# First norm and first dense products in halves of features, squares summed on VectorE and GpSimd, weight splits behind reciprocals: a four-layer diffusion block on one Trainium2 core

## What is computed

```python
def rms_norm(x, gain):
    y = x32 * lax.rsqrt(jnp.mean(x32 * x32, axis=-1, keepdims=True) + EPS)
def modulate_norm(x, gain, shift, scale):
    return rms_norm(x, gain) * (1 + scale) + shift
for i in range(DEPTH):
    mx = jnp.split((silu_c @ ada_w[i] + ada_b[i])[:, None, :], 6, axis=-1)
    hx = modulate_norm(xs, norm_mix[i], mx[0], mx[1])
    ... token mixer: dense products, head norms or convolution, dense product ...
    xs = xs + mx[2] * yx
    hx = modulate_norm(xs, norm_ffn[i], mx[3], mx[4])
    xs = xs + mx[5] * conv_ffn(hx, ffn_w_up[i], ffn_w_dw[i], ffn_b_dw[i], ffn_w_down[i])
```

## Time and profile before

| | |
|---|---|
| median of three runs | 2537.51 us |
| the profiled execution | 2537.72 us |
| its span | 2535.9 us |
| instructions | 35941 |
| TensorE (PE) busy | 2439.2 us, 96% |
| VectorE (DVE) busy | 1808.4 us, 71% |
| ScalarE (ACT) busy | 1044.8 us, 41% |
| GpSimd (POOL) busy | 671.4 us, 26% |
| read from HBM | 334.95 MB, 132 GB/s |

### The profile page before, as it was taken

The page is one execution under the profiler, slowest core; times in us unless marked ns, Lnnn a source line. Parts: engine busy times, 40 slices in busy tenths (PEclk is TensorE's granted clock), DMA queues, the critical chain, the costliest instruction groups (busy, mean ns, idle before and its releaser), DMA issues. The chain is left out here.

```text
span 2535.9 us, 35941 instructions
## 1 busy us (share of the span) xinstructions
PE 2439.2 (96%) x12542; PEld 1994.7 (79%) x12542; DVE 1808.4 (71%) x2642; ACT 1044.8 (41%) x1641; POOL 671.4 (26%) x458
## 2 busy tenths in 40 slices
PE   6998899999999999999999998989999999998999
PEld 4774488888888856788888887868888888767999
DVE  4876559888974344427888768987988876855774
ACT  3335634443232223314444327863544323345443
POOL 5213233332300020032333324854333224101000
PEclk8998999999999999999999999999999999999999
DMA  7542025545633311233555542203455545312555
GB/s 269 180 159 74 1 91 167 174 167 193 220 106 100 101 65 50 83 99 133 174 171 168 179 145 75 67 24 118 169 171 174 185 163 132 109 50 67 184 183 181
DMA packets 94888, 337.46 MB, mean 133 GB/s; under 512 B 11840, under 2 KB 13632, under 8 KB 94656
## 3 DMA queue, kind: packets, MB, share of 16 engines
q1 hardware_dynamic: 67136, 240.38, 28.1%
q10 hardware_dynamic: 24768, 86.74, 10.3%
q0 software_dynamic: 2880, 8.92, 1.7%
HBM read 334.95 MB, written 1.05 MB: 132 GB/s over the span
## 5 line engine op out<-in xcount | busy, mean ns | idle before, releaser
L647 PE MATMUL bank<-Hhi,Whi 128*128 128x512 f32 (+1 forms) x2440 | 873.0, 358 | 29.4 <-DVE Hlo L1535 13.5
L648 PE MATMUL bank<-Hlo,Whi 128*128 128x512 f32 (+1 forms) x2440 | 859.7, 352 | 0.0
L649 PE MATMUL bank<-Hhi,Wlo 128*128 128x512 f32 (+1 forms) x2440 | 859.7, 352 | 0.0
L1448 DVE TENSOR_TENSOR Wlo<-raw,Whi 128x1024 fp32r<-128x1024 f32 x424 | 633.4, 1495 | 253.8 <-ACT Whi L1098 245.0
L1098 ACT ACTIVATE Whi<-raw 128x1024 fp32r<-128x1024 f32 x424 | 448.2, 1059 | 769.6 <-DMA raw<-in_weights 717.6
L647 PEld LDWEIGHTS bank<-Hhi,Whi 128*128 128x128 f32 x2440 | 464.7, 190 | 104.3 <-issue 28.0
L648 PEld LDWEIGHTS bank<-Hlo,Whi 128*128 128x128 f32 x2440 | 465.2, 191 | 64.0 <-issue 3.4
L649 PEld LDWEIGHTS bank<-Hhi,Wlo 128*128 128x128 f32 x2440 | 464.8, 191 | 61.5
L527 POOL TENSOR_TENSOR cond_w<-cond_w,cond 128x1024 f32<-128x1024 f32 x107 | 259.2, 2422 | 621.5 <-DVE square L1472 514.5
L647 PE MATMUL bank<-Ghi,Whi 128*128 128x512 f32 (+1 forms) x770 | 269.1, 350 | 0.0
L649 PE MATMUL bank<-Ghi,Wlo 128*128 128x512 f32 (+1 forms) x770 | 267.1, 347 | 0.0
(11 more groups left out here) (242 smaller groups left out, 2990.7 us busy)
## 6 DMA issues: line engine op xcount, KB each, us to landing
raw<-in_weights SPq DMA_DIRECT2D x424, 512.0 KB, 3.3
cond_w<-in_ada ACTq DMA_DIRECT2D x160, 512.0 KB, 3.9
ada_raw<-in_ada SPq DMA_DIRECT2D x16, 512.0 KB, 15.3
ada_ring<-in_ada SPq DMA_DIRECT2D x16, 512.0 KB, 7.9
rel_in<-in_rpb POOLq DMA_DIRECT2D x48, 128.0 KB, 6.3
decay_t<-in_dist POOLq DMA_DIRECT2D x4, 640.0 KB, 4.2
X<-in_x ACTq DMA_DIRECT2D x1, 2048.0 KB, 10.5
out_y<-X SPq DMA_DIRECT2D x1, 1024.0 KB, 4.8
```

Of the source, the lines that this page charges most:

```text
L647: t.matmul(dst, Whi[:, st.slot, w], hi, start=start, stop=False)
L648: t.matmul(dst, Whi[:, st.slot, w], lo, start=False, stop=False)
L649: return t.matmul(dst, Wlo[:, st.slot, w], hi, start=False, stop=stop)
L1448: v.tensor_tensor(Wlo[:, st.slot, :], raw[:, st.slot, :], Whi[:, st.slot, :].bitcast(F32), ALU.subtract)\
```

## The change

Nothing is computed otherwise; order and places change.

- **Start.** SP loads slices 0 and 2, the four weight slots, then slices 1 and 3. ACT loads the table for Sqrt early and squares all eight chunks into `first_squares`; DVE adds chunks 0 to 3 and POOL 4 to 7 (before: POOL squared and added seven). `first_scale` and `first_chunks` make H for features 0 to 3 from slices 0 and 2; then slices 1 and 3 are stored, and features 4 to 7 follow. TensorE's `first_tiles` does chunks 0 to 3 of four tiles around slices 1 and 3, and chunks 4 to 7 after. Transposes of the identity (`idle_products`) stand where it waits. The banks are FIRST_BANKS, and ACT's QK loop of layer 0 is written out.
- **QK loops:** ACT's root and DVE's `normed` stand ahead of the split of the same step. In layer 0 the ring slice's rows are copied at m = 2 in the first round too.
- **Attention of layer 0:** DVE makes the two late splits one step later; ACT's stay.
- **Retention:** the split for gate tile 4 is done with head 3; TensorE's first o tile waits for each chunk of Y by itself.
- **Convolution:** `diagonals(0)` stands behind Uhi of round 0; 16 `keep_warm` products stand ahead of the last mean, 24 instead of 30 behind it.
- **Last feed-forward:** 8 idle products ahead of `norm_spread`, 10 behind.

```diff
+FIRST_SLICES = (0, 2, 1, 3)
+FIRST_BANKS = (5, 6, 6, 4)
...
-            for q in range(16):
-                sp.dma_start(ada_raw[:, q, :], ada[q, :, :]).then_inc(first_ada[q], 16)
-            for s in range(SLOTS):
-                sp.dma_start(raw[:, s, :], weights[s, :, :]).then_inc(raw_loaded[s], 16)
+            for nth, piece in enumerate(FIRST_SLICES):
+                if nth == 2:
+                    for s in range(SLOTS):
+                        sp.dma_start(raw[:, s, :], weights[s, :, :]).then_inc(raw_loaded[s], 16)
+                for q in range(4 * piece, 4 * piece + 4):
+                    sp.dma_start(ada_raw[:, q, :], ada[q, :, :]).then_inc(first_ada[q], 16)
...
+                pool.wait_ge(first_squared, c + 1)
+                if c > 5:
+                    pool.wait_ge(first_added_too, c - 5)
+                g.tensor_tensor(first_squares[:, c, :], first_squares[:, c - 1, :], first_squares[:, c, :], ALU.add)\
+                    .then_inc(first_added_too, 1)
 
             for layer, p in enumerate(layers):
...
+            def idle_products(count, b=7):
+
+                for n in range(count):
+                    t.transpose(bank[b][:, 0:P], ident[:, :], ident[:, :])
...
+            def first_slice(nth, idle=0):
+                if nth >= 2:
+                    pe.wait_ge(rows_copied, nth)
+                for k in range(C):
+                    q = 4 * FIRST_SLICES[nth] + k // 2
+                    if k % 2 == 0:
+                        idle_products(idle, 3)
+                        pe.wait_ge(first_ada[q], 16)
+                    last = ada_product(bank[FIRST_BANKS[nth]], k, ada_raw[:, q, 512 * (k % 2):512 * (k % 2) + 512])
+                last.then_inc(ada_rows_made, 1)
...
+            def first_tiles(p, steps):
+
+                pe.wait_ge(tile_free, p["mix_tile"] + 4)
+                for k in range(4):
+                    for m in range(2):
+                        first_tile(steps[m], m, (k,))
+                    if k == 1:
+                        first_slice(2)
+                ada_cols(2)
+                first_tile(steps[2], 2, range(4))
+                first_slice(3)
+                first_tile(steps[3], 3, (0, 1))
+                ada_cols(3)
+                first_tile(steps[3], 3, (2, 3))
+                for k in range(4, C):
+                    for m in range(2):
+                        first_tile(steps[m], m, (k,))
+                first_tile(steps[2], 2, range(4, C))
...
-                pe.wait_ge(tile_free, FREE0 + p["mix_tile"] + 48)
                 groups = [[(Step(p["o"] + 2 * m), 8), (Step(p["o"] + 2 * m + 1), 8)] for m in range(C)]
                 for m in range(C - 1):
-                    tile(p["mix_tile"] + 48 + m, m, groups[m], Yhi, Ylo, ALL)
+                    tile(p["mix_tile"] + 48 + m, m, groups[m], Yhi, Ylo, ALL,
+                         (tile_free, FREE0 + p["mix_tile"] + 32) if m == 0 else None)
...
                 for c in range(C):
+                    if c == C - 1:
+                        keep_warm(16)
                     mean_of(c)
...
-                keep_warm(30)
+                keep_warm(24)
...
                 if last_layer:
                     norm_sum(r, tok)
+                    idle_products(8)
                     norm_spread(r, tok)
+                    idle_products(10)
...
+                last.then_inc(cond_spread, 1)
+            first_slice(0)
+            ada_cols(0)
+            pe.wait_ge(cond_ready, 2)
+            first_slice(1, 3)
+            first_norm_sum()
+            ada_cols(1)
+            idle_products(4, 3)
             norm_spread(0, ALL)
-            ada_cols(3)
+            idle_products(8, 3)
```

On ACT and DVE:

```diff
                             act.wait_ge(weights_used, st.n + 1)
                             a.activation(na_sq[:, m % 2, tok], bank[m][:, tok], ACT.Square).then_inc(qk_squared, 1)
-                            split(st)
                             if m:
                                 root_of(m - 1, k - 1, tok)
+                            if layer or st.n:
...
                     a.preload_act_table(ACT.Sqrt)
+                    if h == 3:
+                        split(Step(p["g"] + 1))
...
-                diagonals(0)
                 for c in range(C):
...
                     a.activation(Uhi[:, k, :, CONV_PAD:CONV_PAD + CTX], U[:, k, :, CONV_PAD:CONV_PAD + CTX],
                                  ACT.Copy).then_inc(u_hi, 1)
+                    if c == 0:
+                        diagonals(0)
...
-            square_last(0, ALL)
+            a.preload_act_table(ACT.Sqrt)
             for r in range(2):
                 act.wait_ge(cond_spread, r + 1)
                 for k in range(2):
                     last = a.activation(cond[:, r, 512 * k:512 * (k + 1)], bank[2 * r + k][:, :], ACT.Copy)
                 last.then_inc(cond_ready, 1)
+            act.wait_ge(x_loaded, 16)
+            for c in range(C):
+                a.activation(first_squares[:, c, :], X[:, c, :], ACT.Square).then_inc(first_squared, 1)
+            act.sem_inc(last_squared, 2)
             root_of_norm(0, ALL)
-            for n in range(LEAD):
-                split(Step(n - LEAD))
+            split(Step(-LEAD))
+            split(Step(1 - LEAD))
+            for c in range(C):
+                for half, hs in halves(ALL):
+                    act.wait_ge(norm_scaled, 2 * c + half + 1)
+                    a.activation(Hhi[:, c, hs], ring[(2 * c + half) % 4][:, hs], ACT.Identity,
+                                 bias=mod[:, 0, c, half:half + 1]).then_inc(h_hi, 1)
+                if c < 2:
+                    split(Step(c + 2 - LEAD))
             for layer, p in enumerate(layers):
```

```diff
+            def first_store(nth):
+                dve.wait_ge(ada_rows_made, nth + 1)
+                v.tensor_copy(rows[:, :], bank[FIRST_BANKS[nth]][:, :]).then_inc(rows_copied, 1)
+                ada_store(nth, FIRST_SLICES[nth])
...
+            def first_chunks(first, end, splits):
...
+                for c in range(first, end):
+                    for half, hs in halves(ALL):
+                        n = 2 * c + half
+                        if n >= 4:
+                            dve.wait_ge(h_ready, n - 3)
+                        v.scalar_tensor_tensor(ring[n % 4][:, hs], X[:, c, hs], scale[:, 0, c, half:half + 1],
+                                               spread_bank(0, ALL)[:, hs], ALU.mult, ALU.mult).then_inc(norm_scaled, 1)
+                        if half:
+                            low(n - 1)
+                    low(2 * c + 1)
+                    if c < len(splits):
+                        split(splits[c])
...
-                            if layer == 0 and 0 < n < ADA_QK and m == 2:
+                            if layer == 0 and n < ADA_QK and m == 2:
                                 ada_rows(n)
                             if layer == 0 and n < ADA_QK and m == 3:
                                 ada_store(ADA_START + n)
                             if m:
                                 normed(m - 1, k - 1, i, tok)
+                            if layer or k:
+                                split(Step(p["mix"] + 8 * nth + m, 4, i))
...
-                    if s in LATE_SPLITS[:late]:
-                        split(Step(p["v"] + 8 - late + LATE_SPLITS.index(s)))
+                    if s - 1 in LATE_SPLITS[:late]:
+                        split(Step(p["v"] + 8 - late + LATE_SPLITS.index(s - 1)))
...
                     if h + 1 < RET_HEADS:
                         weighted_scores(h + 1)
+                    if h == 3:
+                        split(Step(p["g"] + 1))
...
-            for s in range(ADA_START):
-                dve.wait_ge(ada_rows_made, s + 1)
-                v.tensor_copy(rows[:, :], bank[5 + s % 2][:, :]).then_inc(rows_copied, 1)
-                ada_store(s)
-                if s == 2:
-                    invert_root(0, ALL)
+            for c in range(1, 4):
+                dve.wait_ge(first_squared, c + 1)
+                if c > 1:
+                    dve.wait_ge(first_added, c - 1)
+                v.tensor_tensor(first_squares[:, c, :], first_squares[:, c - 1, :], first_squares[:, c, :], ALU.add)\
+                    .then_inc(first_added, 1)
+            first_store(0)
+            first_store(1)
+            invert_root(0, ALL)
             dve.wait_ge(const_loaded, CONSTS_IN)
             v.tensor_scalar(qk_gain[:, :, 0:1], qk_gain[:, :, 0:1], NA_HD ** -0.5, None, ALU.mult)
-            for n in range(LEAD):
-                split(Step(n - LEAD))
+            first_scale(0, first_scaled)
+            split(Step(-LEAD))
+            split(Step(1 - LEAD))
+            dve.wait_ge(norm_rstd, upto(0, ALL))
+            first_chunks(0, 4, [Step(n + 2 - LEAD) for n in range(2)])
+            dve.wait_ge(h_ready, C)
+            first_store(2)
+            first_store(3)
+            first_scale(1, scale_ready)
+            first_chunks(4, C, ())
```

130 lines of the change are left out of this document (70 added, 60 removed).

## The result

The changed kernel took 2520.55 us, the median of 4 runs (2519.36 to 2523.92), beside 2537.46 for the kernel before (4 runs). The ratio is 0.9937, with a 95% interval from 0.9919 to 0.9954. A second measurement with five runs gave 2517.83 (2516.41 to 2519.59) against 2537.63, ratio 0.9923 (0.9909 to 0.9936). So it is faster, by 17 to 20 us or 0.6 to 0.8%. The forecast had the sign right and the size too large: 29.9 us were expected, and 2520.55 is at the upper end of the range.

A forecast was written before the change was run, and what follows sets the result against it. TensorE, busy 2439.2 of 2535.9 us, was taken as the bound, leaving 97 us of idleness and half-clock stretches to win. Terms 7.5 + 4.0 + 8.4 + 1.5 + 6.5 + 2.0 = 29.9 off 2537.5 gave 2507.6, range 2499 to 2521.

The forecast's parts named there:

- Start, 7.5: First norm and first four tiles of layer 0: reordered loads, squares and chunks win 7.5 us (1.5 to 11).
- bound of 2: Start: low bound of the gain, 2 us, if TensorE works at half clock between chunk 3 and the second scale.
- rival 1: Start: the second half of the first norm is late, start wins 1.5 to 2, total 2513 us; chance 0.24.
- 0.8 is lost once: Layer 0, tile 4: its split ends at 68.3 while TensorE is ready at 67.5, costing 0.8 us once.
- Late splits, 4.0: Attention of layer 0: VectorE's late splits one step later find Whi ready, winning 4.0 us (1 to 5.5).
- Retention, 8.4: Retention: waits of 1.95 and 3.56 go, and 2.9 of half clock; 8.4 us, high 8.6, low 5.
- Convolution, 1.5: Convolution's last mean: idle products give back 1.0, shorter second sums some 0.5; 1.5 us (0 to 2).
- Layer 3, 6.5: Last attention layer: 3.5 of 4.4 us in two waits go, and 2.9 of half clock; 6.5 us (2 to 6.6).
- 2.35 earlier: Last attention layer: VectorE's reciprocal begins at 2135.6 instead of 2137.95, 2.35 us earlier.
- Last feed-forward, 2.0: Last feed-forward norm: idle products fill two idle stretches, saving half of 4.3 us at half clock; 2.0 us (0 to 2.1).
- Rival 2: Several seams: TensorE's clock stays at half despite idle products and shorter waits, losing 10.5 us, total 2518; chance 0.10.
- Rivals 3 and 4: QK loops: late splits make it slower, 2544 us, chance 0.02; seams: gains waited for at the next, 2535, chance 0.02.

The follow-up runs named there:

- The best version: Changed kernel without slice 2's idle products, head sum and ring copy earlier, GpSimd's second bias batch later, convolution's diagonals and last mean as before; 2516.41 us, ratio 0.9916.

## Why the prediction was right or wrong

**Start, 7.5: the wrong term.** The step that failed is "TensorE has work in every gap from 31 on, and idle products in front of it", by which I stayed at the worked-out 8.0 and not at the bound of 2 that the same paragraph gives for a half clock. I treated rows of TensorE as free because it idled before. Four sizes were off. They were read in one execution of a start that varies by 4.3 us between executions, so of the 5.5 that are missing only the parts that recur can be called causes:

- *The norm sum at 23.8* came at 24.0 but lasted until 25.95, ahead of which stood 12 idle products and columns that waited 1.51 for DVE's copy, as DVE was adding squares. 1.5 us, shown by taking these 12 products out: the first dense product came at 30.5 to 31.0 in all four kernels without them, and at 32.4 to 34.9 in all eight with them.
- *The clock.* 0.50 and 0.58 from 28 to 42, where I counted full speed. Worth up to 2.7 us; that it varies is shown, what sets it is not. The "bound of 2" was written for this case.
- *Second scale at 50.0, tile 3 at 66.0* came at 52.40 and 70.15. This is rival 1 in kind: slice 3 stands in the queue behind products at half clock, though chunk 4 came at 52.6 and not at its 56. Its 1.5 to 2 for the start is what the first profile shows, 2.0.
- *"0.8 is lost once"* for tile 4: 1.8 us from the end of tile 3 to tile 4 in the kernel before became 3.8. About 0.9 of the 2.0 is a head sum that stood ahead of the end of tile 3 before and stands behind it now, which the comparison of 66.0 with 74.06 left out. The rest is the waits for the ring's copy and for ACT's square of tile 3. The best version, with head sum and copy moved, reaches tile 4 1.2 us sooner after the first head sum.

**Late splits, 4.0: right.** 3.65, and 3.85 back when undone. "6.3 less 2.3" should have been 6.3 less 2.5, for two splits of 1.23, which gives 3.8. The wide products of these steps stayed 12.8 and 12.2 apart, not "11 us apart throughout": a split still stands in each.

**Retention, 8.4: right.** 8.2, and all three parts are seen: no 1.95, no 3.56, full clock behind. Undoing the second part gave 5.4 and not the expected 6.5, since half clock lasted less long there.

**Convolution, 1.5: wrong by 3.3.** Of these 0.9 is the wait for "issue" at the norm behind retention, 0.8 the diagonals, and 1.5 the gain that was taken back. "Sixteen products ahead of it give back half, 1.0" is right for the mean (1.12 for 2.08). "The sums behind the shorter second run some 0.5" is not: the clock fell later, and six products and a spread took back what the mean had won. "I take nothing" for the diagonals was a wrong sign too: they stand ahead of the second sigmoid on ACT, DVE waits 4.04 for it, and TensorE's 7.0 us wait for Wlo at 1559.93 comes behind that (5.1 in two waits before, 3.8 in two with the diagonals moved back). Moving them back won 0.7.

**Layer 3, 6.5: 4.1.** The step that failed counted one split twice: "2.35 earlier" at the head of DVE's chain and "one split fewer" at its end are the same split. From its first reciprocal to the last awaited QK the chain took 63.0 us before and 63.4 after, 13 splits in both. What is left is a chain that begins 1.8 earlier relative to TensorE's first head sum (the "2.35 earlier") and takes 0.4 longer, and the stretch gained 1.4. The half clock behind the wait went and the next stretch gained 2.7, near the forecast 2.9, but this was in part luck: the half clock also stayed away in the kernel with the old order, behind 2.56, and two kernels with the new order won only 1.2 there. I had taken it for a sure follower of such a wait.

**Last feed-forward, 2.0: right**, 1.9, and 1.7 back when undone.

**The rivals.** Rival 1 (0.24) is what the start did, in size and partly in kind. Alone it gave 2513; the 5 to 7.5 us beyond it are the convolution (3.3), layer 3 (2.4) and small ones. Rival 2 held for the start and the convolution, and not for the places that carry most of it. Rivals 3 and 4 did not happen: no wait for Wlo longer than 2 us stands in the QK loops, and gains did not vanish at later seams.

**The split beside GpSimd.** In the QK loops splits beside GpSimd's additions took 1.35 (at 70.30) to 2.03 us instead of 1.22. Timeline of POOL and DVE in layer 3 of the changed kernel:

```profile
2120.40 1.00 POOL L570 TENSOR_TENSOR rel<-rel_in,mask 128x384 f32<-128x384 f32 x1
...
2120.45 2.03 DVE L1525 TENSOR_TENSOR Wlo<-raw,Whi 128x1024 fp32r<-128x1024 f32 x1 [3.41 <-ACT Whi L1163]
```

The addition ends at 2121.40 and the split at 2122.48, 1.08 later, nearly a whole split. That holds throughout: 95 of the 424 splits of the changed kernel took more than 1.27 us, each began while a GpSimd instruction ran, and each ended 1.07 to 1.09 us after that instruction's end, up to 3.06 us long. The other thirteen traces show the same, within 1.07 to 1.10. So a split makes hardly any headway while a GpSimd instruction that began ahead of it runs. This is what the prediction cited from the Trainium skill, "SBUF — State Buffer", section "SBUF: two separate sides", that the loser of the shared port "fully blocks", and the trace agrees. What did not come is its price of 3.8 for the start: it counted three whole additions of 1.26, and a split loses only what is left of the one in hand, 0.13, 0.70 and 0.61 us at the three splits ahead of V that lost anything.

## What to carry to other kernels

Work out a start as a queue for every engine, with idle products, copies and head sums in it as instructions with a price: an engine that idled for 5.8 us before is no longer free once its work comes early. When one move is said to help at the head and at the tail of a chain, count the instructions between the two ends in both orders before adding. The edits that took whole waits away from the attention of layer 0 and from retention gave what was worked out for them; the idle products around the convolution's small matmuls gave nothing that could be measured. And execute the same code several times before a stretch is given a price: the start's 2.0 lies in a spread of 4.3.

## What was not expected of the hardware

- The same instructions were granted 0.50, 0.61 or 1.00 of the clock from 32 to 36 us in three executions, with up to 2.7 us between them at V, and 4.3 over five executions.
- Pieces of 512 KB asked for together with GpSimd's loads of 128 KB landed after 7.8 to 15.2 us (medians of ten executions), and after 6.1 and 6.8 in the two kernels where these were held back. It mattered who asked first: 7.8 where SP was 1.1 us ahead of GpSimd, 9.2 to 10.8 where both began within 0.4 us, 15.2 where it was 1.1 behind.
- A weight split on VectorE that met a running GpSimd instruction ended 1.07 to 1.10 us after it, in all 1326 cases of the fourteen traces.
- Behind a wait of 1.44 in layer 3, and of 2.56 in another kernel, the first matmul took 0.47 us and the next ones 0.39, full clock; behind 2.57 in the kernel before the first took 0.77.
- The waits put down to "issue" at the three norms repeat to about 0.1 when a kernel is run again and differ by up to 1.3 us at one place between kernels whose code there is the same.
